# Moving the splits of the next stage's first weight tiles behind the norms and the routings, with more spare products in the routings

## What is computed

```python
# first block, two layers
for l in range(2):
    x = x + hybrid_mixer(rms_norm(x, norm_mix[l]), ...)      # w_in 1024x2048, conv, gating, w_out 1024x1024
    h = rms_norm(x, norm_ffn[l])
    x = x + (swiglu(h, ...) if l == 0 else moe_swiglu(h, ...))  # width 2816; 8 experts, the best 2 of each token
x = rms_norm(x, norm_final)
# second block
h = rms_norm(x, attn_norm_g)
proj = h @ w_in                                   # q, k, v, gates, short convolution, attention
x = x + merged @ w_o
x = x + hierarchical_moe(rms_norm(x, ffn_norm_g), ...)   # 4 groups of 4 experts: best group, best 2 in it
x = x + sigmoid(rms_norm(x, ple_norm_g) @ w_pg) * (p @ w_ple)
```

## Time and profile before

| | |
|---|---|
| time, median of 3 runs | 1628.16 us (1625.53 to 1629.66) |
| the profiled execution's own time | 1627.02 us |
| its span, first to last instruction | 1625.3 us |
| mean granted clock of TensorE | 0.989 |
| TensorE busy | 1571.9 us, 97% |
| VectorE busy | 1261.2 us, 78% |
| ScalarE busy | 1015.4 us, 62% |
| read from memory | 436.5 MB, 273 GB/s over the span |

### The profile page before, as it was taken

The page is one execution under the profiler, slowest core; times in us unless marked ns, Lnnn a source line. Parts: engine busy times, 40 slices in busy tenths (PEclk is TensorE's granted clock), DMA queues, the critical chain, the costliest instruction groups (busy, mean ns, idle before and its releaser), DMA issues.

```text
span 1625.3 us, 23325 instructions
## 1 busy us (share of the span) xinstructions
PE 1571.9 (97%) x9200; PEld 1379.1 (85%) x9200; DVE 1261.2 (78%) x1111; ACT 1015.4 (62%) x888; POOL 63.8 (4%) x81
## 2 busy tenths in 40 slices
PE   9999999999899999999999999998989999999998
PEld 8979999898788788888878888786879989889986
DVE  6985444599788888888888888888876764778886
ACT  4663444455577777777777777776654454457763
POOL 4000000000100000000000000002000000000010
PEclk9999999999999999999999999999999999989999
DMA  9635555543498999999999999999976435559990
GB/s 275 231 104 194 182 190 190 167 141 104 156 373 304 390 390 338 389 345 389 342 394 384 351 387 344 389 350 391 392 261 195 153 107 169 179 188 353 363 372 27
DMA packets 244795, 444.66 MB, mean 274 GB/s; under 512 B 12116, under 2 KB 122224, under 8 KB 244720
## 3 DMA queue, kind: packets, MB, share of 16 engines
q1 hardware_dynamic: 239488, 426.17, 74.1%
q0 software_dynamic: 3744, 13.12, 2.3%
q10 hardware_dynamic: 1488, 4.34, 0.8%
HBM read 436.52 MB, written 7.09 MB: 273 GB/s over the span
## 4 chain that ended last, share of the span: by engine, by line
PE 73%; DMA 8%; DVE 8%; issue 6%; ACT 5%; POOL 0%; DVEq 0%; ACTq 0%; SPq 0%; POOLq 0%
PE PS L1210 22%; PE PS L1212 21%; PE PS L1211 21%; DMA ring<-in_moe_wu_dram 5%; DVE w_low L1762 3%; ACT w_high L920 3%; PE PS L1299 2%; DMA ring<-in_moe_wd_dram 1%; DMA work<-h_rows_kept,row_no 1%; DVE h L1787 1%; PE PS L1509 1%; PE PS L1428 1%; DVE hT_low L1762 1%; ACT w_high L753 0%; DVE work L1929 0%
## 5 line engine op out<-in xcount | busy, mean ns | idle before, releaser
L1762 DVE TENSOR_TENSOR w_low<-ring,w_high 128x2048 fp32r<-128x2048 f32 (+1 forms) x403 | 919.2, 2287 | 248.2 <-ACT w_high L753 129.8
L920 ACT ACTIVATE w_high<-ring 128x2048 fp32r<-128x2048 f32 x306 | 585.1, 1917 | 203.2 <-PE PS L1212 164.5
L1210 PE MATMUL PS<-w_high,hT_high 128*128 128x512 f32 (+1 forms) x1184 | 416.0, 351 | 10.4 <-DVE w_low L1762 9.1
L1212 PE MATMUL PS<-w_high,hT_low 128*128 128x512 f32 (+1 forms) x1184 | 410.8, 347 | 0.0
L1211 PE MATMUL PS<-w_low,hT_high 128*128 128x512 f32 (+1 forms) x1184 | 410.6, 347 | 0.0
L753 ACT ACTIVATE w_high<-ring 128x2048 fp32r<-128x2048 f32 (+1 forms) x97 | 183.0, 1893 | 129.3 <-PE PS L1212 119.5
L1210 PEld LDWEIGHTS PS<-w_high,hT_high 128*128 128x128 f32 x1184 | 224.5, 190 | 41.3 <-DVE w_low L1762 12.4
L1212 PEld LDWEIGHTS PS<-w_high,hT_low 128*128 128x128 f32 x1184 | 224.5, 190 | 28.1
L1211 PEld LDWEIGHTS PS<-w_low,hT_high 128*128 128x128 f32 x1184 | 224.7, 190 | 26.5
L1210 PE MATMUL PS<-hT_high,w_high 128*128 128x256 f32 x832 | 240.3, 289 | 3.4 <-DVE hT_low L1762 2.3
L1211 PE MATMUL PS<-hT_low,w_high 128*128 128x256 f32 x832 | 236.2, 284 | 0.0
(11 more groups left out here) (343 smaller groups left out, 1158.3 us busy)
## 6 DMA issues: line engine op xcount, KB each, us to landing
ring<-in_moe_wg_dram SPq DMA_DIRECT2D x88, 1024.0 KB, 10.7
ring<-in_moe_wu_dram SPq DMA_DIRECT2D x88, 1024.0 KB, 10.5
ring<-in_moe_wd_dram SPq DMA_DIRECT2D x80, 1024.0 KB
ring<-in_w_in_dram SPq DMA_DIRECT2D x36, 1024.0 KB, 6.1
ring<-in_w_gate_dram SPq DMA_DIRECT2D x16, 1024.0 KB, 8.2
ring<-in_w_up_dram SPq DMA_DIRECT2D x16, 1024.0 KB, 7.5
ring<-in_w_down_dram SPq DMA_DIRECT2D x16, 1024.0 KB
ring<-in_ffn_wg_dram SPq DMA_DIRECT2D x11, 1024.0 KB, 5.3
```

Source lines behind the costliest of these rows:

```text
L920: act.activation(w_high[:, (s.base + k) % SPLITS, :], slot(w), ACT.Copy).then_inc(s.high_taken, 1)
L1210: mm(o, left_high, right_high, start=first, stop=False, skip_group_check=shared)
L1212: return mm(o, left_low, right_high, start=False, stop=last_one, skip_group_check=shared)
L1762: return tt(out_, whole, part.bitcast(F32), ALU.subtract)
```

## The change

High splits (ScalarE): of the two that stood at the end of each mixer one is left. In layer 0 the second and third tiles of the dense stage are split at norm 1's end. In layer 1 the second and third tiles of the first experts are split behind the exponential of routing 1; for the second experts the third is split behind that of routing 2.

Low splits (VectorE): dense's first tile is split behind the first add of norm 1, ahead of ms, instead of ahead of the add. Mixer 1's second tile is split behind norm 2. The first tile of the first experts, which was split ahead of norm 3, and the first two of the second experts, which were split ahead of norm 6, go into the list `lead`, behind the choice of slots.

TensorE: in norms 3 and 6 three spare products behind the transposes of the first row tile and seven behind those of the second. In both routings 16 spare products directly behind the transposed logits, without waiting for `exps_wanted`, instead of 5 and 8 behind that wait; and 8 instead of 4 behind the rank products.

```diff
--- before.py
+++ after.py
@@ -894,7 +894,6 @@
                 conv_std(1)
                 second_silu()
                 high(B + 12)
-                high(B + 13)
 
             def dense(B):
                 act.wait_ge(small_landed, 16 * 14)
@@ -1032,12 +1031,15 @@
             norm(0, between=0, tile=1)
             high(2)
             mixer(0, BASE[0])
-            norm(1, tile=BASE[1] + 2)
+            norm(1, tile=BASE[1] + 1)
+            high(BASE[1] + 2)
             dense(BASE[1])
             norm(2, tile=BASE[2] + 2)
             mixer(1, BASE[2])
-            norm(3, tile=BASE[3] + 2)
+            norm(3)
             route_exps(1, EXPERTS)
+            high(BASE[3] + 1)
+            high(BASE[3] + 2)
             sweeps(moe1, main1, rest1, restream1, 1, BASE[4])
             norm(5, tile=BASE[4] + 1)
             B = BASE[4]
@@ -1137,8 +1139,9 @@
             high(B + 27)
             high(B + 28)
             high(B + 29)
-            norm(6, tile=B + 30)
+            norm(6)
             route_exps(2, 20)
+            high(B + 30)
             sweeps(moe2, main2, rest2, restream2, 2, BASE[6] + 1)
             B = BASE[6]
             norm(7, tile=B + 2)
@@ -1187,6 +1190,8 @@
                             last = nc.tensor.transpose(PS[:, 2 * t + b, c * P:(c + 1) * P],
                                                        h[:, t, (4 * b + c) * P:(4 * b + c + 1) * P], ident[:])
                         last.then_inc(h_turned, 1)
+                    if n in (3, 6):
+                        spare(4, (3, 7)[t])
 
             whole = []
 
@@ -1410,8 +1415,7 @@
                 pe.wait_ge(routes_low, 3)
                 small_columns(0, pair, ne)
                 small_turned(2, ne, 2 * k - 1)
-                pe.wait_ge(exps_wanted, k)
-                spare(4, (5, 8)[k - 1])
+                spare(4, 16)
                 pe.wait_ge(mask_ready, k)
                 m = [mk[:, t, 0:groups] for t in range(TT)]
                 mm(PS[:, 1, 0:groups], above[:], m[0], start=True, stop=True)
@@ -1419,7 +1423,7 @@
                 mm(PS[:, 1, groups:2 * groups], above[:], m[1], start=False, stop=True)
                 mm(PS[:, 1, 2 * groups:3 * groups], ones[:], m[0], start=True, stop=False)
                 mm(PS[:, 1, 2 * groups:3 * groups], ones[:], m[1], start=False, stop=True).then_inc(rank_ready, 1)
-                spare(4, 4)
+                spare(4, 8)
 
             def gather_half(e, s, b):
 
@@ -1853,10 +1857,12 @@
                 if tile is not None:
                     low(tile)
 
-            def rows_and_norm(n, b, half, name):
+            def rows_and_norm(n, b, half, name, tile=None):
 
                 v.wait_ge(rows_half, half)
                 tt(x[:, 0, :], x[:, 0, :], bank(b, 2), ALU.add).then_inc(x_updated, 1)
+                if tile is not None:
+                    low(tile)
                 v.wait_ge(sumsq_ready, SUMMED[n] + 1)
                 ts(ms[:, 0:1], ss[:, 0:1], 1.0 / D, EPS, ALU.mult, ALU.add).then_inc(ms_ready, 1)
                 for hf, a in enumerate(HALVES_OF_ROW):
@@ -2005,8 +2011,7 @@
                 low(B + 11)
                 second_scale()
                 second_rest()
-                low(B + 12)
-                rows_and_norm(2 * l + 1, 4, HALF_MIX[l], ((l, "out_conv"), 1))
+                rows_and_norm(2 * l + 1, 4, HALF_MIX[l], ((l, "out_conv"), 1), B + 12 if l == 0 else None)
                 if l == 0:
                     low(B + 13)
                     low(B + 14)
@@ -2021,12 +2026,13 @@
                     if kind == "u":
                         v.wait_ge(silu_ready, j + 1)
                         tt(wk[2 + j % 2][:, 0:512], wk[j % 2][:, 0:512], bank(2 + j % 2), ALU.mult).then_inc(hid_ready, 1)
-                    if p < 3 * HALVES - 1:
+                    if p < 3 * HALVES - 2:
                         low(B + p + SPLITS)
                     if kind == "u":
                         v.wait_ge(hid_taken, j + 1)
                         rest_of(hid_low[:, j % 2, :], wk[2 + j % 2][:, 0:512], hid_high[:, j % 2, :]).then_inc(hid_low_ready, 1)
                 rows_and_norm(2, 4, HALF_FFN, ("ffn", "d", HALVES - 1))
+                low(BASE[2] + 1)
                 low(BASE[2] + 2)
 
             def places(values, rows_, n, dst):
@@ -2328,7 +2334,7 @@
             mixer(1, BASE[2])
             later = route()
             B = BASE[4]
-            sweeps(moe1, main1, rest1, restream1, 1, later, [BASE[3] + 1, BASE[3] + 2])
+            sweeps(moe1, main1, rest1, restream1, 1, later, [BASE[3], BASE[3] + 1, BASE[3] + 2])
             two_norms()
             low(B)
             low(B + 1)
@@ -2484,13 +2490,13 @@
             merge(3)
             merged_low(2)
             merged_low(3)
-            for T in range(26, 30):
+            for T in range(26, 28):
                 low(B + T)
             rows_and_norm(6, 4, HALF_O, ("o", 3))
             later = route2()
             first = BASE[4] + 30
             B = BASE[6]
-            sweeps(moe2, main2, rest2, restream2, 2, later, [first], B + 1)
+            sweeps(moe2, main2, rest2, restream2, 2, later, [first - 2, first - 1, first], B + 1)
             norm(7, tile=B + 2)
             low(B + 3)
             low(B + 4)
```

## The result

The changed kernel takes 1614.88 us (median of 4 runs, 1613.31 to 1616.26); the kernel before took 1627.03 (4 runs, 1625.53 to 1629.66) beside it. The ratio is 0.9923 (95% interval 0.9906 to 0.9941). In the profiled execution of the changed kernel (own time 1614.74) the span is 1613.0 us and the mean granted clock 0.997; before, 1625.3 and 0.989.

A forecast was written before the change was run, and what follows sets the result against it. TensorE held 73% of the chain, the rest mostly its waits for norms and routings; 4.86 us (norms) + 4.64 (routings) = 9.5 off 1627.0 gives 1617.5, plus 1.14 for the median: 1618.7 us, range 1615.5 to 1624.5 (0.86).

The forecast's parts named there:

- The norms: Norms 1, 2, 3 and 6: adds start behind the twelfth product, gaining 0.60 + 1.22 + 1.58 + 1.46 = 4.86 us.
- The fourth rival: Norms: something else holds the adds, so only the routings gain; 1623.6 us, chance 0.04.
- The routings: Both routings: clock kept, first expert tile earlier by 1.66 us in routing 1 and 2.98 in routing 2, sum 4.64.
- The first rival: Routings: the clock still falls; in one about 1622.1 us (chance 0.09), in both 1625.5 (chance 0.06).
- The ring: SP's load queue: ring slots refilled too late, one to three tiles at 2.7 us, 1621.4 to 1626.8 us; chance 0.07.
- The third rival: Norm before each routing: clock falls ahead of the logits, spares run at 0.27 us each; +5.9 us, 1634; slower had 0.04.
- The step that failed: Norm 1: the chance that the 0.6 us shift keeps its clock, up to 2 us more, was left to the range.
- theory A: From the experiments: splits and spares do what the sum says; the excess is norm 1's clock, falling in some executions of either kernel.
- a second step: Whole kernel: 1.14 us added to 1617.5, as the median of three runs, 1628.16, stood above the profiled execution.
- theory B: From the experiments: edits have effects the sum lacks; norm 1's moved work keeps its clock, or spares do more than shown.

## Why the prediction was right and where it failed

**The norms.** Right in place and in size: adds 0.03 us behind the twelfth product's end, ms behind the split at norm 1, gains of 0.84, 1.21 (with the clock set aside), 1.65 and 1.49. At norm 1 the forecast was low by 0.24 us, of which some is scatter ahead of the norm: averaged over five profiles before and two after, the gain of that stretch is 0.62. The fourth rival (adds not released early) is out.

**The routings.** 1.68 and 3.02 us against 1.66 and 2.98, with the clock at 1.00 and the wait for the two splits as forecast. The split of these sums was less exact: the spares alone gave 2.54 and 3.88, and the second split behind the choice takes back 0.85, not 0.4. The two errors cancelled in the net, because where two chains end close together the net is set by VectorE's chain alone, and that was costed from its rows.

**The clock in the routings.** The first rival is out for the changed kernel, and it seems to have been priced too high: with the clock lost in both (no sixteen) the two stretches take 1.9 and 1.5 us longer, 3.4 in all, where it had 6.8 more, though there the fall ended before the second gather; with the first gather alone slow, 0.78. It put the four spares and the slow gathers on the path in full and forgot that the splits cover part of them, though the same paragraph of the sum had said so.

**The ring.** Out in the changed kernel: a slot is refilled at 424.85, sooner than the 430 forecast, and from the first expert tile to the last product on token_no, in the seventh trip, it takes 596.2 us, before 596.6 to 597.1. A late load did cost 1.3 to 1.9 us in three of the other kernels, but at the end of the last trip, some 700 us behind the place that the rival names.

**The other side.** The third rival is out: sixteen transposes from 410.68 with the clock at 1.00 from 405 to 428. The Trainium skill, "TensorE: Matmul & The Clock Gate", Part 4 (PE-mode transpose), says that the full clock doesn't engage in transpose mode. The windows of norms 3 and 6 don't agree. Falls among the logits were seen in two kernels without the turn's spares, in routing 2 alone; but all five profiles of the kernel before had transposes with no spares between them at norm 3 and kept the clock through its logits.

**The step that failed** is this one: "The chance that norm 1 keeps its clock by the 0.6 us shift (up to 2 us more) lies in the forecast's own range." The fall was taken as a property of the kernel before, and its absence as an outside chance of the changed one. It is one of the execution, and theory A holds for it: with norm 1's work as before it fell in three profiles and held in four (spares alone among them); with norm 1's edit and no spares in its turn it held in five of eight. In the three where it fell the fall came later, from 121 instead of 119, and cost 1.5 us. Its row in the kernel without the sixteen, which has the changed kernel's norm 1, and then the row of the spares alone, which has the old norm 1:

```profile
121.00:125.00 4.00, 3.96 (x20) 3.96 (x21) 3.22 (x3) 3.65 (x5) 0.00 (x0) 0.57 0.38 131
...
121.00:125.00 4.00, 3.38 (x28) 3.38 (x29) 4.00 (x4) 2.43 (x5) 0.00 (x0) 1.00 0.43 135
```

So the pair compared, fallen before and held after, differs by 1.8 us that no edit made. The sum, which started from an execution with the fall in it, had nothing for this; the sentence names it, but hands it to a range whose low end lay 3.2 us below the centre.

That width would have been enough, had a second step held: 1.14 us were added because the median of three runs stood above the profiled execution. In the changed kernel's four runs the median stands 0.14 above the profiled execution; with that offset the same width would have begun at 1614.5. Over 55 runs of the kernel before the median is 1627.35, 0.33 above it, so 0.8 of the 1.14 were chance. From 1618.7 to 1614.9 the 3.8 us are: norm 1's clock 1.8, this offset 1.0, the stretch of the first experts and attention 0.8, the start 0.2. None of the three smaller ones was in the forecast, and none is larger than the spread of its own stretch or of the runs.

**What stays open.** A held norm 1 is about as likely in either kernel, so over many executions its 1.8 us should mostly cancel; the medians of 55 and 10 runs still differ by 11.4 us, and the means by 12.3, where the sum has 9.5. Averaged over the five profiles of the kernel before and the two of the changed one the difference is 11.7: above the forecast are norm 1's clock with 0.8 us (two of five against none of two), the longer routing 1 of one profile with 0.4, the stretch of the first experts with 0.8 and the last with 0.9; norm 2's fall in one takes back 0.7. Each of these is no larger than the spread of its own stretch (the first tile of the second experts to the end is 187.0 to 189.7 us in the five). A gain of 9.5 us is a ratio of 0.9942, at the edge of the two intervals of the changed kernel (0.9906 to 0.9941 and 0.9909 to 0.9943). So theory B isn't excluded for the spares: by their stretches they give 6.4 us, by the means 8.1, with an interval from 5.2 to 10.6. Nor was it settled why the load at the end of the last trip comes late in some of the last kernels tried, nor whether that and the fall in their second experts are chance; one profile of each can't tell.

## What to carry to other kernels

Cost each edit at the wait that ends last, and where two engines' chains end close together, make the sum for both: that gave the routings to 0.04 us, though TensorE's own chain there was 0.4 us off. Before a clock fall in a short stretch goes into a sum, look at several executions: a term that comes and goes belongs in the range of both kernels, not in the difference. A wait of an engine that is otherwise full is worth filling where short products stand behind it, but an earlier first tile counts only as far as the tiles behind it come sooner too: of 0.84 us about half was lost there.

## What the runs showed of the hardware

The granted clock of the same code differs from one execution to the next. Norm 1 of the kernel before ran at 0.50 (1.2 GHz) in two profiles and at 1.00 (2.4 GHz) in three, with the adds ahead of it within 0.3 us of one another; norm 2, which held in all five of these, fell in the second profile of the changed kernel. The Trainium skill, "TensorE: Matmul & The Clock Gate", Part 1 (The HAM clock gate (the "warmup" mystery)), says that the cold start of one kernel varies from run to run, because what watches the engine runs freely of the kernel. The profiles agree that it varies, and show it in the middle of a kernel; the reason no run here shows.

One fall was there every time, the one with the longest row of waits and short products ahead of it: both routings of the kernel before in five profiles of five. Sixteen spare products without a wait kept it away in every profile that had them together with the turn's and eight behind the ranks. What the spares buy is large beside what they do: 8.1 us of the 12.5, and the time at half clock from some 36 to some 15 us.
